# mLSTM memory pieces decayed by two engines, and the RWKV samples' memory products placed inside the inversion, in a two-layer recurrent decoder trunk

## What is computed

```python
num = g_inter[..., None] * jnp.einsum('bhtd,bhde->bhte', qc, C) + jnp.einsum('bhts,bhse->bhte', s, vc)
C = dec[..., None, None] * C + jnp.einsum('bhs,bhsd,bhse->bhde', ws, kc, vc)
h = ((h - mu) * lax.rsqrt(var + MH_EPS)).reshape(B, T, D_B).astype(dt) * mh_g
```

```python
sa = jnp.einsum('bhvk,bhk->bhv', S, -kk_t)
S = S * w_t[:, :, None, :] + sa[..., None] * (kk_t * a_t)[:, :, None, :] + v_t[..., None] * k_t[:, :, None, :]
```

## Time and profile before

| what | value |
|---|---|
| median of 3 runs | 1521.6 us (1521.47 to 1523.23) |
| the profiled execution, its own time | 1519.59 us |
| its span, first to last instruction | 1517.9 us |
| PE busy, share of the span | 1464.3 us, 96% |
| DVE, ACT, POOL busy | 985.0, 695.9, 378.2 us |

### The profile page before, as it was taken

How to read it: one execution, slowest core, us unless ns; L and a number is a source line. 1 busy time by engine, 2 the same in 40 slices (tenths; PEclk the granted TensorE clock), 3 DMA queues, 4 the chain that set the end, 5 groups by cost and what they waited for, 6 DMA issues and landing times.

```text
span 1517.9 us, 33992 instructions
## 1 busy us (share of the span) xinstructions
PE 1464.3 (96%) x13374; PEld 1409.3 (93%) x13374; DVE 985.0 (65%) x1579; ACT 695.9 (46%) x1188; POOL 378.2 (25%) x407
## 2 busy tenths in 40 slices
PE   7999999999989999999999999989999899999995
PEld 7999998899867999999999999979998689999995
DVE  4444435588476687775577776466865777877644
ACT  5333334765645543334443334366565465333332
POOL 4222363010532422220412222300115323222100
PEclk9999999999999999999999999999999999999998
DMA  8544543443214555444544545434521444555351
GB/s 221 150 144 149 168 149 88 126 128 101 55 34 134 157 160 151 146 141 150 159 137 142 151 152 156 152 88 123 129 78 33 123 121 136 165 150 167 126 166 35
DMA packets 318938, 198.82 MB, mean 131 GB/s; under 512 B 7792, under 2 KB 303760, under 8 KB 318832
## 3 DMA queue, kind: packets, MB, share of 16 engines
q1 hardware_dynamic: 315120, 190.69, 43.1%
q0 software_dynamic: 3712, 6.62, 2.1%
HBM read 188.50 MB, written 8.78 MB: 130 GB/s over the span
## 4 chain that ended last, share of the span: by engine, by line
PE 85%; DVE 7%; ACT 3%; issue 2%; DVEq 1%; DMA 0%; POOL 0%; SPq 0%; POOLq 0%; ACTq 0%
PE bank L2120 24%; PE bank L2122 23%; PE bank L2121 23%; DVE wlo L2613 2%; PE bank L2207 1%; DVE rlo L2644 1%; ACT whi L2410 1%; ACT z L1183 1%; PE bank L2212 1%; PE bank L764 1%; PE bank L752 1%; DVE raw L1578 1%; PE bank L2171 1%; PE bank L853 1%; PE bank L458 1%
## 5 line engine op out<-in xcount | busy, mean ns | idle before, releaser
L2410 ACT ACTIVATE whi<-raw 128x1024 fp32r<-128x1024 f32 x340 | 358.2, 1059 | 471.9 <-PE bank L2122 455.7
L2613 DVE TENSOR_TENSOR wlo<-raw,whi 128x1024 fp32r<-128x1024 f32 x340 | 421.2, 1243 | 230.1 <-ACT whi L2410 229.3
L2120 PE MATMUL bank<-rhi,whi 128*128 128x322 f32 x984 | 306.5, 311 | 0.0
L2122 PE MATMUL bank<-rhi,wlo 128*128 128x322 f32 x984 | 305.9, 311 | 0.0
L2121 PE MATMUL bank<-rlo,whi 128*128 128x322 f32 x984 | 304.8, 310 | 0.0
L2120 PE MATMUL bank<-xh,whi 128*128 128x320 f32 x912 | 286.2, 314 | 4.6 <-DVE xl L2787 3.5
L2121 PE MATMUL bank<-xl,whi 128*128 128x320 f32 x912 | 283.0, 310 | 0.0
L2122 PE MATMUL bank<-xh,wlo 128*128 128x320 f32 x912 | 282.9, 310 | 0.0
L2882 POOL TENSOR_TENSOR hl<-scratch,hh 128x320 f32 x88 | 146.9, 1669 | 495.4 <-DVE scratch L2734 379.7
L2120 PE MATMUL bank<-hh,whi 128*128 128x320 f32 (+1 forms) x704 | 218.4, 310 | 0.5 <-DVE wlo L2613 0.5
L2121 PE MATMUL bank<-hl,whi 128*128 128x320 f32 (+1 forms) x704 | 217.4, 309 | 0.0
(11 more groups left out here) (421 smaller groups left out, 1888.8 us busy)
## 6 DMA issues: line engine op xcount, KB each, us to landing
raw<-in_ffn_wg SPq DMA_DIRECT2D x88, 512.0 KB, 3.8
raw<-in_ffn_wu SPq DMA_DIRECT2D x88, 512.0 KB, 3.8
raw<-in_ffn_wd SPq DMA_DIRECT2D x88, 512.0 KB, 3.6
raw<-in_w_in SPq DMA_DIRECT2D x60, 512.0 KB, 3.8
raw<-in_w_out SPq DMA_DIRECT2D x16, 512.0 KB, 6.1
raw<-in_state_C SPq DMA_DIRECT2D x8, 512.0 KB, 6.1
out_s_C<-raw SPq DMA_DIRECT2D x8, 512.0 KB, 4.1
ring<-in_state_wkv POOLq DMA_DIRECT2D x8, 256.0 KB, 5.5
```

The source lines that it names most:

```text
L2120: pe.matmul(out, w_hi, hi, start=start, stop=False)
L2122: return pe.matmul(out, w_lo, hi, start=False, stop=stop)
L2410: act.activation(whi[:, slot, :], raw[:, slot, :], ACT.Copy).then_inc(hi_ready.sem, 1)
L2613: dve.tensor_tensor(wlo[:, slot, :], raw[:, slot, :], whi[:, slot, :].bitcast(F32), ALU.subtract).then_inc(lo_ready.sem, 1)
```

## The change

- **Decay by ACT.** For C1, C3, C5 and C7, ACT multiplies the old memory by its decay in place (`head_decay`, four activations with a per-partition scale, at steps 19 to 22), and DVE adds the product in one operation of 512 columns.
- **Sample means later.** `head_means` of the samples moves from step 20 to 21, its squares 20 to 21, spreads 21 to 22, roots 22 to 23, scaling 23 to 24. The table load moves from step 18 to 16.
- **POOL masks early.** The first masked values get a buffer of their own (over bk) and are formed before the memset of qm, and so before the loads. The decay diagonals wait for the gate columns instead of the third score tile.
- **Memory products in the inversion.** All four go behind the pieces of steps 25 and 26, two in each, into bank 7. ACT copies them at c = 0. The samples' r then comes at c = 1 and their u at c = 2; y stays at c = 3.

```diff
-        vmask = [area(1536, SB, DK, of=spare), area(15304, SB, DK)]
+        vmask = [area(9480, SB, DK), area(15304, SB, DK)]
...
+        DECAYED = (1, 3, 5, 7)
...
-            sums = bank[3][:, :].rearrange("p (j s t) -> p j s t", j=NJ, s=2)
+            sums = bank[7][:, :].rearrange("p (j s t) -> p j s t", j=NJ, s=2)
...
-                    if c == 1:
-                        samples_memory_products(pe, L, 1)
                     if c == 2:
-                        samples_memory_products(pe, L, 3)
-                    if c == 3:
                         samples_u(pe, L)
...
                 if c == 1:
-                    samples_memory_products(pe, L, 2)
-                if c == 2:
                     samples_r(pe, L)
...
-                if c == 0:
-                    samples_memory_products(pe, L, 0)
...
+                if n in OWN_AT:
+                    for j in range(NJ // 2):
+                        samples_memory_products(pe, L, 2 * OWN_AT.index(n) + j)
...
+        OWN_AT = (25, 26)
...
+        def head_decay(act, L, i):
+
+            h, half = 2 * (i // 4) + i % 2, i // 2 % 2
+            act.wait_ge(num_mm.sem, num_mm.by(L, NTT))
+            for s in range(4 * half, 4 * half + 4):
+                at = h * TS + s * ST + ST - 1
+                last = act.activation(C0[:, h, s, :], C0[:, h, s, :], ACT.Copy, scale=rexp[:, at:at + 1])
+            last.then_inc(heads_decayed.sem, 1)
...
+                if c == 0:
+                    act.wait_ge(samples_mm.sem, samples_mm.by(L, 1))
+                    act.activation(s0sum[:, :, :, :].rearrange("p j s t -> p (j s t)"), bank[7][:, :],
+                                   ACT.Copy).then_inc(s0sum_ready.sem, 1)
                 if c == 2:
-                    act.wait_ge(samples_mm.sem, samples_mm.by(L, 1))
-                    act.activation(s0sum[:, :, :, :].rearrange("p j s t -> p (j s t)"), bank[3][:, :],
-                                   ACT.Copy).then_inc(s0sum_ready.sem, 1)
-                if c == 3:
                     act.wait_ge(samples_mm.sem, samples_mm.by(L, 3))
...
-                if n == SQUARES_AT[0] + 1:
+                if n == WEIGHTS_AT[2] + 2:
                     act.preload_act_table_set("sqrt_and_others")
                 if n in ROOTS_AT:
                     head_roots(act, L, ROOTS_AT.index(n))
+                if n in DECAYS_AT:
+                    head_decay(act, L, DECAYED[DECAYS_AT.index(n)])
...
-        SQUARES_AT = (17, 20)
-        ROOTS_AT = (19, 22)
+        SQUARES_AT = (17, 21)
+        ROOTS_AT = (19, 23)
+        DECAYS_AT = (19, 20, 21, 22)
...
-                for k in range(4):
+                if i in DECAYED:
+                    own = C0[:, h, 4 * half:4 * half + 4, :].rearrange("p b e -> p (b e)")
+                    dve.wait_ge(heads_decayed.sem, heads_decayed.by(L, DECAYED.index(i) + 1))
+                    last = dve.tensor_tensor(own, own, b[:, :], ALU.add)
+                for k in range(0 if i in DECAYED else 4):
...
-                if c == 3:
+                if c == 2:
                     dve.wait_ge(samples_mm.sem, samples_mm.by(L, 3))
...
-                if c == 2:
+                if c == 1:
                     dve.wait_ge(samples_mm.sem, samples_mm.by(L, 2))
                     tt(rsb_s[:, :, :], heads4(bank[3]), yr[:, slot(NPC), :, :], ALU.add).then_inc(rs_ready.sem, 1)
...
-        MEANS_AT = (17, 20)
-        SPREADS_AT = (19, 21)
-        SCALED_AT = (20, 23)
+        MEANS_AT = (17, 21)
+        SPREADS_AT = (19, 22)
+        SCALED_AT = (20, 24)
...
             pool.wait_ge(kv_ready.sem, kv_ready.by(L, 2 * NTT))
+            masked_values(pool, L, 0)
             pool.memset(qm[:, :, :], 0.0).then_inc(qm_zero.sem, 1)
...
-            pool.wait_ge(tile_mm.sem, tile_mm.by(L, NTT))
+            pool.wait_ge(cols_turned.sem, cols_turned.by(L, 1))
...
-            pool.wait_ge(side_copied.sem, side_copied.by(L, copied_by_scalar(RVS)))
-            masked_values(pool, L, 0)
             pool.wait_ge(num_mm.sem, num_mm.by(L, NTT))
             masked_values(pool, L, 1)
```

More of the change, by code:

```diff
@@ L364, in hymba_kernel @@
         h_ready = signal("h_ready", 2)
+        heads_decayed = signal("heads_decayed", 4)
         vmask_ready = signal("vmask_ready", HB // 2)
```

## The result

The changed kernel takes 1530.32 us (median of 20 runs, 1524.24 to 1532.98), the kernel before 1522.33 (20 runs, 1517.76 to 1527.73): a ratio of 1.0041, 95% interval 1.003 to 1.0052. The forecast was 1516.3, with a range from 1513 to 1522.5. The profiled execution of the changed kernel took 1532.98; its span is 1531.2 us against 1517.9.

The account below looks back on a forecast made before the run. PE, with 85% of the chain of waits, was taken to set most of the time. Two layers of 0.1 + 0.87 and 3.32 of pauses, 5.26 us, took the median from 1521.6 to 1516.3; range 1513 to 1522.5.

Parts of the forecast that it names:

- POOL masks early: Steps 16 to 19: moving POOL's first masks earlier gains 0; delaying POOL's queue costs 0, bounds 0 to 1.0 for a lock.
- My sum: Whole kernel: two layers of 0.1 (inversion) + 0.87 (recurrence), and 3.32 of pauses, 5.26 us gained.
- the prediction's own signs of being wrong: A pause over 1 us remains, PE idles for DVE over 1 us after H1, or inversion length changes over 1 us.
- The new order stalls: Rival: ACT's decays or POOL's locks hold DVE over 1.5 us a layer where PE waits; above 1524.6; chance 0.06.
- Products: Inversion, behind C6 and C7: four groups take 3.5 us uncovered, 1.8 for two; the inversion ends 0.1 earlier.
- PE's clock falls in the stretch that is now PE's: Rival, steps 21 to 24: half clock recurs uncovered, pauses kept, 3.4 us lost in two layers, 1523.1; chance 0.12.
- Recurrence: Recurrence: without the products, the hand-off intervals between PE and DVE shorten by 0.87 us a layer, pauses apart.
- Pauses: Recurrence: PE's issue pauses in both layers vanish once the dense products leave, -1.76 and -1.56 us, bounds 0 to all.
- The pauses stay: Rival, recurrence: pauses belong to the program's place or weights' traffic; only 1.94 us gained, 1519.7; chance 0.25.
- Decay, means and H1: Inversion, steps 19 to 25: cheaper, earlier pieces let H1 end at 444.3 and C6 and C7 start 3.6 us earlier.
- the 0 to 1.0 of lock that I took as 0: Inversion: POOL's memory keys may meet the prompt's or samples' scaling, 0 to 1.0 us a layer, counted as 0.
- Range: Whole kernel: the time lies from 1513 to 1522.5 us, with 0.18 chance of falling outside.

Follow-up runs that it names:

- E7: The kernel before with only ACT's decay and the later means with earlier table load: 1517.63 us, ratio to before 0.9959.
- E3: The changed kernel with the decay diagonals late again and the samples' products back in the recurrence: 1518.0 us, ratio to before 0.9971.
- E1: The changed kernel with only the decay diagonals moved back behind the third score tile: 1524.03 us, ratio to before 1.0002.
- E2: The changed kernel with only the samples' products back in the recurrence: 1522.64 us, ratio to before 0.9997.
- E4: The kernel before with only the samples' products moved into steps 25 and 26: 1527.33 us, ratio to before 1.003.
- E11: The kernel before with only ACT's decay of C1, C3, C5, C7: 1520.49 us, ratio to before 0.9991.
- E12: The kernel before with only the samples' means later and the table load earlier: 1527.72 us, ratio to before 1.0039.
- E9: E7 plus an unread second copy of the four thin products in steps 25 and 26: 1530.24 us, ratio to before 1.0047.
- E10: E7 plus unread wide 128x128 identity products in steps 25 and 26, same PE length as E9's filler: 1523.57 us, ratio to before 1.0007.
- E6: E1 plus unread wide 128x128 identity products at four places in the recurrence: 1525.57 us, ratio to before 1.0005.
- E8: The kernel before again, with no edit, for a second profile: one run, 1520.74 us.
- E5: E1 plus an unread second copy of the four products at their old places in the recurrence: 1530.59 us, ratio to before 1.0045.

## Why the prediction was wrong, step by step

From E7 over E3 and E1 the ratios give the change in pieces: decay and means -0.41%, early masks +0.12% (inside the intervals), products +0.31%, diagonals +0.39%, together +0.41%. In us: -6.2, +1.8, +4.7, +5.9. My sum had -7.2, 0, +2.0 and 0. In another order the last two differ: E2 against E3 gives the diagonals +4.0, the changed kernel against E2 the products +6.7.

Two of the prediction's own signs of being wrong bear on this. The pauses did go, but the end of the inversion is 4.2 and 2.9 us longer than before, where more than 1 was to mean a mistake.

- **Diagonals: the step "POOL masks early" failed.** "price 0, bounds 0 to 1.0 for a lock there" weighed L1896 alone. The other half of that point of the change, the diagonals' new wait, has no term in the sum: that it brings them ten us up, to where DVE forms the prompt's queries, was not followed to L1482. Measured 3.83 and 3.97 instead of 0.68, 3.6 to 4.0 us a layer on the path with the half clock behind the lock, 4.0 to 5.9 us in all (E2 to E3, the changed kernel to E1). The rival "The new order stalls", at 0.06, named POOL's locks and a time above 1524.6; of the rivals it came nearest, though the diagonals are not in it either. In the kernel before this same pair had met lightly: with the diagonals at 422.82 a query operation took 0.89 instead of 0.41. The Trainium skill (SBUF — State Buffer, SBUF: two separate sides) says that a DVE operation with two SBUF inputs and a POOL operation that reads SBUF take a port pair as an exclusive lock for a whole instruction. That agrees in kind, but one POOL instruction is 1.05 us here, and DVE was held for three of them, which the section does not lead one to expect.
- **Products: length right, clock left out.** Two groups were to take 1.8: 1.80, but the other two took 3.53. They lie on the path, as forecast. What the sum lacks is half clock where PE is last: 6 to 16 us of it at the end of the inversion in each of the six layers of the changed kernel, E1 and E4, against 0 to 3.6 in the profiles of before, E3 and E7. The products are not the only thing that does it: E11 and E12 without them have 2.4 to 10.6. Nor do E3 and E7 escape the fall. It comes 25.5 to 28.6 us after the start of the reduction of step 17 there, and 25.0 to 27.4 after it in the changed kernel and E1; with the products in the inversion PE then still has work that nothing covers, and without them the recurrence is about to begin, where half clock costs less (E7's took 23.73 with 10.7 us of it, the first of before 21.49 with none). By the means the products also make it longer, by 8 us an execution (55.6 in E1 against 47.3 in E3, 58.4 in E4 against 50.8 before). What makes the clock fall at that place stays open; E9 and E10 show that the kind of work there matters. The rival "PE's clock falls in the stretch that is now PE's" had the mechanism and the sign, at 0.12, but put it between steps 21 and 24, after waits, and at 3.4 us in both layers together; it came in steps 25 and 26, with PE recorded as busy all the time from 448 on, and lasts into the recurrence. The Trainium skill (TensorE: Matmul & The Clock Gate, What's actually happening) has "the default state is throttled, and activity releases the throttle"; the records show PE busy for all of 457 to 465, with the clock at 0.50 from 457.75 on, so busy in the records is not the same thing.
- **Recurrence: right only at full clock, by an estimate.** I expected 21.4 - 0.87 - 1.7 = 18.9. It took 21.05 in both layers of the changed kernel, 0.4 less than before, with 7.6 us at half clock, and 19.91 (E1's first layer, E4) with some 4; along these the full-clock value is about 18.7.
- **Pauses: the forecast holds.** No pause over 0.5 us in the recurrences of the changed kernel, E1, E4 and E6, and not for half clock alone: E4's have 4 us of it and no pause, E8's 3.4 and 6.8 and both pauses. So the rival "The pauses stay" is out. With the products in the recurrence there are pauses of 1.15 to 2.76 us in all recurrences that ran mostly at full clock (before, E8, E10, E11, E2's first layer; in E12's second layer between two falls), and none where 10 us or more of it ran at half clock (E3, E5, E7, E9). Dense issue at full speed goes with the pause; that it is instruction supply stays my reading, and wasn't tried by itself. I take the pause to be one reason why half clock costs so little there: over the runs of the kernel before, 24 us more half clock went with 5 us more time.
- **Decay, means and H1: right in direction, short by 1.1 us in the first layer.** By the old count means here that 2.74 is taken off, the delay with which the changed kernel reaches the reduction of step 17. The table load moved, but the numerators' copy, at 439.07, waits for ACT's copy of the growth from 438.53 and ends 0.7 earlier by the old count, not 1.3. The prompt's scaling begins at 439.97, and its second operation took 0.63, not 0.17, beside POOL's memory keys (the 0 to 1.0 of lock that I took as 0):

```profile
439.97 0.20 DVE L1572 RECIPROCAL scratch<-scratch 128x8 f32<-128x8 f32 x1 [0.98 <-ACT scratch L1154]
440.25 0.63 DVE L1574 TENSOR_TENSOR scratch<-scratch 128x8 f32<-128x8 f32 x1
...
443.13 0.68 DVE L1588 TENSOR_TENSOR raw<-raw,bank 128x512 f32<-128x512 f32 x1
```

  By the old count C6 and C7 (452.85) stand at 450.1 instead of 449.0, 2.5 earlier than in the earlier trace rows and not 3.6. From H1's end to there it took 4.7, as forecast. The addition at 0.68 and four activations at 1.26 are as forecast, L1530's successor at 0.15 as well.
- **Range.** The sum was set against one profile, and the clock of that profile (0.986) was taken as the kernel's own. The runs of before lie between 0.979 and 0.991.

## What to carry to other kernels

When an instruction moves on a queue, follow every instruction that moves with it, and look beside each at its new time for a DVE operation with two SBUF operands. Before moving small matrix products to another place, ask what they do to PE's clock there, and test it with work of the same length that nothing reads, once thin and once wide. E7, the change without its products and without POOL's new order, is the version to keep.

## Not expected of the hardware

A stretch of half clock of 10 to 20 us can follow work that the records show as busy, and whether and where it comes differs between executions of one kernel (E8). A wide filler of 3.4 us a layer lowered the half clock of the whole execution from 45.8 to 36.8 us (E7, E10). One DVE instruction can be held through three POOL instructions in a row, even where it is recorded as starting 0.2 to 0.8 us ahead of them (3.83, 3.97 and 4.36 us); once, 0.74 ahead, it got through in 0.80.
